# Sparse attention with split values stationary and split, scaled, turned probabilities moving

## The reference, cut to what matters

```python
o_cmp, p_cmp = nsa_compressed(q, kv[:, :, 0], kv[:, :, 1], ...)      # 31 compressed keys
o_slc = nsa_selected(q, kv[:, :, 2], kv[:, :, 3], top_i, top_ok)
o_win = nsa_window(q, kv[:, :, 4], kv[:, :, 5])
gb = jax.nn.sigmoid(g_nsa.reshape(B, S, NSA_GROUPS, NSA_HPG, 3))
y_nsa = (gb[..., 0:1] * o_cmp + gb[..., 1:2] * o_slc + gb[..., 2:3] * o_win).reshape(B, S, NSA_Q)
```

## Time and profile before

| | |
|---|---|
| median of 3 runs | 2828.78 us |
| span of the profiled execution | 2832.2 us |
| PE busy | 2781.4 us (98%) |
| DVE busy | 2007.5 us (71%) |
| ACT busy | 1158.5 us (41%) |
| POOL busy | 62.7 us (2%) |
| chain that ended last | PE 75%, DVE 20%, issue 3%, ACT 1% |
| granted PE clock | 9 or more tenths in all 40 slices |

### The profile page before, as it was taken

The page is one execution under the profiler, slowest core; times in us unless marked ns, Lnnn a source line. Parts: engine busy times, 40 slices in busy tenths (PEclk is TensorE's granted clock), DMA queues, the critical chain, the costliest instruction groups (busy, mean ns, idle before and its releaser), DMA issues.

```text
span 2832.2 us, 41533 instructions
## 1 busy us (share of the span) xinstructions
PE 2781.4 (98%) x16782; PEld 2473.6 (87%) x16782; DVE 2007.5 (71%) x2956; ACT 1158.5 (41%) x1635; POOL 62.7 (2%) x22
## 2 busy tenths in 40 slices
PE   7999999999999999999999999999999999999998
PEld 7888888888888989789898899988999888789897
DVE  4456654544658969589694797875979588669794
ACT  4333444444243424334344443432434357434342
POOL 0000011111000000000000000000000000000000
PEclk9999999999999999999999999999999999999999
DMA  7223312222533333223333233332332343123322
GB/s 221 90 78 105 112 62 84 93 81 97 184 120 98 103 107 111 104 89 105 105 105 106 79 101 109 100 114 69 109 111 93 122 171 110 60 75 107 112 95 75
DMA packets 262192, 295.39 MB, mean 104 GB/s; under 512 B 6210, under 2 KB 248018, under 8 KB 259342
## 3 DMA queue, kind: packets, MB, share of 16 engines
q1 hardware_dynamic: 257008, 281.53, 30.3%
q10 hardware_dynamic: 5022, 11.57, 1.1%
HBM read 276.30 MB, written 16.78 MB: 103 GB/s over the span
## 4 chain that ended last, share of the span: by engine, by line
PE 75%; DVE 20%; issue 3%; ACT 1%; DMA 0%; DVEq 0%; ACTq 0%; SPq 0%
PE bank L1420 13%; PE bank L1422 12%; PE bank L1421 12%; PE bank L1863 5%; PE bank L1865 5%; PE bank L1864 5%; PE bank L1694 5%; PE bank L1752 2%; DVE gate_quarters_lo L2625 2%; DVE up_quarters_lo L2625 2%; PE bank L2026 1%; PE bank L1742 1%; DVE w_lo L2121 1%; PE bank L1435 1%; PE bank L1436 1%
## 5 line engine op out<-in xcount | busy, mean ns | idle before, releaser
L2121 DVE TENSOR_TENSOR w_lo<-w_raw,w_hi 128x2048 fp32r<-128x2048 f32 (+2 forms) x140 | 306.4, 2191 | 138.9 <-ACT w_hi L831 135.7
L1420 PE MATMUL bank<-hid_hi,w_hi 128*128 128x512 f32 x880 | 343.0, 390 | 0.0
L1421 PE MATMUL bank<-hid_lo,w_hi 128*128 128x512 f32 x880 | 342.5, 389 | 0.0
L1422 PE MATMUL bank<-hid_hi,w_lo 128*128 128x512 f32 x880 | 342.4, 389 | 0.0
L831 ACT ACTIVATE w_hi<-w_raw 128x2048 fp32r<-128x2048 f32 (+2 forms) x134 | 243.0, 1820 | 240.0 <-PE bank L1422 161.3
L1420 PE MATMUL bank<-h_hi,w_hi 128*128 128x512 f32 x752 | 298.6, 397 | 3.0 <-DVE w_lo L2121 1.4
L1421 PE MATMUL bank<-h_lo,w_hi 128*128 128x512 f32 x752 | 293.0, 390 | 0.0
L1422 PE MATMUL bank<-h_hi,w_lo 128*128 128x512 f32 x752 | 292.9, 390 | 0.0
L1422 PEld LDWEIGHTS bank<-hid_hi,w_lo 128*128 128x128 f32 x880 | 165.2, 188 | 34.5
L1421 PEld LDWEIGHTS bank<-hid_lo,w_hi 128*128 128x128 f32 x880 | 165.3, 188 | 33.7
L1420 PEld LDWEIGHTS bank<-hid_hi,w_hi 128*128 128x128 f32 x880 | 165.2, 188 | 33.8
(11 more groups left out here) (465 smaller groups left out, 6962.4 us busy)
## 6 DMA issues: line engine op xcount, KB each, us to landing
w_raw<-in_ffn_w_in_dram SPq DMA_DIRECT2D x88, 1024.0 KB, 5.0
w_raw<-in_ffn_w_out_dram SPq DMA_DIRECT2D x32, 1024.0 KB, 5.2
w_raw<-in_w_in_dram SPq DMA_DIRECT2D x28, 1024.0 KB, 5.1
w_raw<-in_w_ffn_in_dram SPq DMA_DIRECT2D x22, 1024.0 KB, 5.0
w_raw<-in_ffn_w_out_dram SPq DMA_DIRECT2D x16, 768.0 KB, 4.5
w_raw<-in_conv_w_pw_dram SPq DMA_DIRECT2D x12, 1024.0 KB, 6.6
phase_taps<-in_conv_dw_phases_dram SPq DMA_DIRECT2D x10, 1152.0 KB, 7.8
w_raw<-in_w_ffn_down_dram SPq DMA_DIRECT2D x8, 1024.0 KB, 5.2
```

Source lines behind the costliest of these rows:

```text
L1420: nc.tensor.matmul(bank[b][:, 0:n], wh, xh, start=first, stop=False)
L1421: nc.tensor.matmul(bank[b][:, 0:n], wh, xl, start=False, stop=False)
L1422: ins = nc.tensor.matmul(bank[b][:, 0:n], wl, xh, start=False, stop=last)
L2121: v.tensor_tensor(w_lo[slot][:, 0:n], raw[s][:, 0:n], w_hi[slot][:, 0:n].bitcast(F32), ALU.subtract).then_inc(w_lo_ready, 1)
```

## The change

The order of steps becomes query block, branch, head, so that the 8 steps of a query block (both branches) are neighbours. PE works in 18 slots of a pair of steps (two heads): scores of pair j, `GATES_IN_SLOT[j]` gates matmuls, turn of pair j-1, weigh of pair j-2.

- Values: split in high and low parts after their projection (units 10 and 11), stored to DRAM, and loaded again for each group as `v_hl`, high and low columns side by side, 128 stationary columns.
- Probabilities: DVE scales each by the reciprocal of its sum times its gate before the transposes (`scale_step`). ACT copies the turned ones as the high part, DVE subtracts for the low part (`high_of_pair`, `low_of_pair`); the first 8 pairs (512 and 384 keys) head by head, the last 8 pair by pair.
- `weigh`: values stationary, 256 columns (two heads) of the turned high or low parts moving, fp32r. All of a query block's steps and its compressed branch add up in one bank, feature-major, with the sums of the high and of the low value columns in different partition halves.
- Compressed branch: scores from 16 matmuls of 64 columns (both key parts beside each other, no gates matmul between), scaled before its transposes; for each query block 4 transposes, a copy, and one matmul of 512 columns. Three DVE additions replace others (`cmp_add`, `cmp_parts`, `cmp_values`).
- Each block's halves are added by ACT and DVE (`move_half`, `add_halves`) and split (`y_of_block`, `y_low`). `out_step`, `y_tok`, its transposes and the multiply-adds are gone.
- ACT's high part of the second weight unit comes in slot 2, and that of the next group's first unit after the last block and `gate_evac(4)`. SP loads q and keys when the last mask step has its scores, and the values behind the group's last `add_halves`.

```diff
-STEPS = [(br, qb, hh) for br in range(2) for qb in reversed(range(TT)) for hh in range(HPG)]
+STEPS = [(br, qb, hh) for qb in reversed(range(TT)) for br in range(2) for hh in range(HPG)]
+GATES_IN_SLOT = (16, 8, 8, 8, 6, 6, 6, 6, 6, 5, 5, 5, 5, 5, 5, 5, 10, 10)
+GATE_EVAC = {2: 0, 6: 1, 10: 2, 15: 3}
+SECOND_GATE_UNIT = 2
...
+                def weigh(j):
+                    br, qb, hh = STEPS[2 * j]
+                    pe.wait_ge(s_pl, g * COPIES + (2 * j + 2 if j < NARROW else NARROW + j + 1))
+                    out_ = bank[ACC_BANK[j // 4 % 2]][:, P * hh:P * (hh + 2)]
                     for kb in range(qb + 1):
+                        keys = slice(kb * P, (kb + 1) * P)
+                        nc.tensor.matmul(out_, v_hl[:, br, kb, :], pT_hi[j % 2][:, :, keys], start=j % 4 == 0 and kb == 0, stop=False)
+                        ins = nc.tensor.matmul(out_, v_hl[:, br, kb, :], pT_lo[j % 2][:, :, keys], start=False, stop=False)
                     ins.then_inc(s_o, 1)
...
+                for j in range(PAIRS + 2):
+                    if j < PAIRS:
+                        scores(2 * j)
+                        scores(2 * j + 1)
+                    gates(GATES_IN_SLOT[j])
+                    if j == 2:
+                        pe.wait_ge(m_lo_s, 4)
+                        pe.wait_ge(vd_landed, g * 32 + (VD_LANDED + 32))
+                    if 1 <= j <= PAIRS:
+                        turn(j - 1)
+                    if j >= 2:
+                        weigh(j - 2)
+                    if j % 4 == 0 and j > 0:
+                        cmp_turn(j // 4 - 1)
+                    if j % 4 == 1 and j > 1:
+                        cmp_weigh(j // 4 - 1)
                 gates(GATE_TILES * 3 * KT)
...
+                def scale_step(i):
+                    br, qb, hh = STEPS[i]
+                    n = P * (qb + 1)
+                    dve.wait_ge(s_e, g * NS + (i + 1))
+                    link(v.reciprocal(prec[:, i:i + 1], psum_row[:, i:i + 1]))
+                    v.tensor_scalar(prob[i % 4][:, 0:n], prob[i % 4][:, 0:n], prec[:, i:i + 1], g_gate[:, qb, hh, br + 1:br + 2],
+                                    ALU.mult, ALU.mult).then_inc(s_c, 1)
...
+                for j in range(PAIRS + 2):
+                    if j < PAIRS:
+                        mask_step(2 * j)
+                        mask_step(2 * j + 1)
+                        if j == 0:
+                            cmp_add(0)
+                        scale_step(2 * j)
+                        if j == 0:
+                            cmp_add(1)
+                        scale_step(2 * j + 1)
+                    if j == 0:
+                        cmp_shift()
+                    if 1 <= j <= PAIRS:
+                        low_of_pair(j - 1)
+                    if j == 2:
+                        cmp_gain()
+                    if j == 3:
+                        cmp_scale()
+                        cmp_parts(0)
+                        cmp_values()
+                    if j == 5:
+                        compressed_keys(g + 1)
+                    if j in (6, 10, 14):
+                        cmp_parts(j // 4)
+                    if j in (7, 11, 15):
+                        add_halves(j // 4 - 1)
+                    if j in (8, 12, 16):
+                        y_low(j // 4 - 2)
```

More of the change, by code:

```diff
@@ L205 @@
 K_END = 1656
-NSA_PER = 25
+NSA_PER = 50
 class Chain:
@@ L1025, in _ @@
             act.sem_inc(gt_copied, 2)
-            for s in range(2):
-                act.sem_inc(gt_stored[s], 16)
+            act.sem_inc(gt_stored, 16)
             def q_store(n):
@@ L1097, in _ @@
                             high_in_loop(g * 2 + (U_NSA // 2 + 1), 1, 1, HALF)
[L1098 to L1102 removed]
+                move_half(TT - 1)
+                y_of_block(TT - 1)
+                gate_evac(4)
@@ L1772, in _, with turn @@
-                pe.wait_ge(q_stored, 16 * GROUPS)
-                pe.wait_ge(c_p, g + 1)
+                    out_, q = bank[S_BANK[i % len(S_BANK)]][:, 0:n], q_st[:, hh, qb * P:(qb + 1) * P]
+                    nc.tensor.matmul(out_, q, k_st[br][0][:, 0:n], start=True, stop=False)
+                    nc.tensor.matmul(out_, q, k_st[br][1][:, 0:n], start=False, stop=True).then_inc(s_s, 1)
+                def turn(j):
+                    n = P * (STEPS[2 * j][1] + 1)
+                    if j > NARROW + 1:
+                        pe.wait_ge(s_pl, g * COPIES + (NARROW + j - 1))
+                    for e in range(2):
+                        i = 2 * j + e
+                        pe.wait_ge(s_c, g * NS + (i + 1))
+                        if 1 <= j < NARROW:
+                            pe.wait_ge(s_pl, g * COPIES + (2 * (j - 1) + e + 1))
+                        if j in (NARROW, NARROW + 1) and e == 0:
+                            pe.wait_ge(s_pl, g * COPIES + (2 * NARROW - 1 + j - NARROW))
+                        b, c = (PT_BANK[e], 0) if j < NARROW else (PT_BANK[j % 2], n * e)
+                        for kb in range(n // P):
+                            ins = nc.tensor.transpose(bank[b][:, c + kb * P:c + (kb + 1) * P], prob[i % 4][:, kb * P:(kb + 1) * P], ident)
+                        ins.then_inc(s_t, 1)
@@ new lines, in cmp_turn, with cmp_weigh @@
+                def cmp_turn(k):
+                    pe.wait_ge(c_p, g * TT + (k + 1))
+                    pe.wait_ge(y_sum, g * TT + (k + 1))
+                    for hh in range(HPG):
+                        ins = nc.tensor.transpose(bank[ACC_BANK[(k + 1) % 2]][:, hh * P:(hh + 1) * P],
+                                                  c_hl[:, hh:hh + 2, :, :].rearrange("p h a n -> p (h a n)").bitcast(F32), ident)
+                    ins.then_inc(c_t, 1)
+                def cmp_weigh(k):
+                    pe.wait_ge(c_ta, g * TT + (k + 1))
+                    pe.wait_ge(vc_ready, g + (VC_READY + 1))
+                    nc.tensor.matmul(bank[ACC_BANK[k % 2]][:, :], vc_st[:, :], pT_c[:, :], start=False, stop=True).then_inc(acc_ready, 1)
@@ L1774, in _ @@
+                pe.wait_ge(q_landed, g * 16 + 16)
+                pe.wait_ge(kc_ready, g + 1)
                 for qb in range(TT):
                     for hh in range(HPG):
[L1776 to L1784 removed]
@@ L1785, in _ @@
-                ins.then_inc(c_o, 1)
-                gates(12)
-                pe.wait_ge(y_done, g + 1)
-                for t in range(2):
-                    for qb in range(TT):
-                        ins = nc.tensor.transpose(bank[6 + t][:, qb * P:(qb + 1) * P], y_tok[:, qb, t * P:(t + 1) * P], ident)
-                    ins.then_inc(y_turned, 1)
+                        c = 2 * NCP * (2 * qb + hh // 2)
+                        ins = nc.tensor.matmul(bank[PT_BANK[hh % 2]][:, c:c + 2 * NCP], q_st[:, hh, qb * P:(qb + 1) * P],
+                                               kc_st[:, :, :].rearrange("p a n -> p (a n)"), start=True, stop=True)
```

377 lines of the change are left out of this document (188 added, 189 removed).

## The result

The changed kernel takes 2860.36 us (median of 4 runs, 2859.76 to 2863.43) against 2829.32 (4 runs, 2825.6 to 2831.51): ratio 1.0114, 95% interval 1.0102 to 1.0127. It is 31 us slower, where 12 faster was forecast. The time lies outside the range; "slower" had a chance of 0.20.

A forecast was written before the change was run, and what follows sets the result against it. PE bounded the kernel before, DVE would after: 61.1 slots + 9.3 boundary, 72.3 with crossings, + 5.6 holds = 77.9 us a group; merge 12.1 us earlier, 2828.8 - 12 = 2817 us, range 2786 to 2842.

The forecast's parts named there:

- slower: Rival, chance 0.20: POOL's subtractions hold DVE for all their 13.9 us a group, giving 2850 us.
- The merge: Work behind the attention's four groups: forecast to start at 672.7 against 684.8, 12.1 us earlier.
- the boundary between groups: Behind DVE's slot 15, DVE waits for PE's gates, last turn, weighings and first scores: 9.3 us a group.
- POOL's holds: POOL's subtractions delay DVE's scalings: 3.3 us in slot 2, 1.3 in slot 7, 1.0 at group start; 5.6 a group.
- DVE's slots: DVE's masks, scalings and low parts in slots 0 to 15, plus its compressed-branch work: 61.1 us a group.
- PE's saving: Cheaper weighing 8.1, compressed output 3.1, compressed scores 1.8, dropped transposes 0.9: 13.9 us a group.
- the 77.9: Forecast time in us of one attention group: 72.3 for DVE's chain with crossings, plus 5.6 of holds.
- PE-bound: Rival, chance 0.08: DVE's waits for ACT overlap better, PE sets the time at 68.2 us a group, 2778 us.
- P: The time of one attention group in us, entering the forecast merge start as 361.1 + 4P.
- no hold: Rival, chance 0.16: POOL doesn't hold DVE's scalings, 72.3 us a group, 2794 us.
- PE's waits for POOL inside the groups: Late low weights stall PE 2.4 us a group at slot 0's gates, hidden under DVE's longer slot.
- the 0.40: Chance given to the forecast itself, 2817 us with scalings held by POOL; own range 2805 to 2824.

The follow-up runs named there:

- e1: The changed kernel with POOL's four subtractions a group cut from 2048 or 1024 columns to 64: 2814.66 us, ratio 0.9953.
- e11: e10 with DVE's program for the four groups written out instead of looped: 2809.7 us, ratio 0.9923 against the kernel before.
- e5: The changed kernel with each gates tile doing its 16 high-weight products first, then the 8 low-weight ones: 2851.25 us, ratio 1.0068.
- e13: e11 with POOL making the low weights again and no subtraction on DVE: 2826.25 us, ratio 0.9983.
- e10: The changed kernel with low-weight products last, ACT's high parts earlier, gates matmuls moved to early slots, low weights made by DVE: 2827.26 us, ratio 0.9986.
- e8: The kernel before with POOL's low-weight subtractions in the attention loop cut to 64 columns: 2827.61 us, ratio 0.9985.
- e14: The kernel before with low-weight products last in each gates tile and DVE's loop written out: 2827.96 us, ratio 0.9992.
- e9: The changed kernel with only DVE's loop over the four groups written out: 2859.02 us, ratio 1.0101.
- e3: The changed kernel with ACT making the fourth unit's and the next group's first high parts earlier, POOL kept: 2845.89 us, ratio 1.0057.
- e2: The changed kernel with the four low-weight subtractions a group made by DVE and none by POOL: 2840.39 us, ratio 1.004.

## Why the prediction was wrong

The merge was laid at 672.7 and began at 711.7, 39 us later. Experiment e1 splits that in two halves. Without POOL the forecast's own terms give 356.0 + 4 x 72.3 = 645.2; e1 has its merge at 665.7: 20.5 us. POOL was priced at 4 x 5.6 + 5.1 = 27.5 us; it costs 711.7 - 665.7 = 46.0: 18.5 us. The steps that failed in the sum are therefore two: the boundary between groups (9.3 us laid, 13.3 measured in e1) and POOL's holds (5.6 us a group laid, 10.4 to 11.1 measured). The sum went by DVE's slots and the boundary; PE's saving is in it only through the boundary.

- **PE's saving, 13.9 us a group: too large**, though the 77.9 wasn't added up from it. Adding up distances from start to start, PE's own pieces are 81.8 us of a group before and 72.7 in e1: 9.1. The price inside a run of weighings was right, 0.12 us apart, but its ends cost more (0.20 for the first), so that 80 take 12.0 us and not 9.2: 4.8 saved, not 8.1. The compressed output takes 0.42 for each matmul of 512 columns and 64 rows, not 0.23: 2.5 saved. Compressed scores and the gates between them save 4.1 (0.4 and 3.7) where 1.8 was laid. The transposes of `y_tok` save 1.0. Against that, scores are 2.4 and turns 0.8 dearer beside their new neighbours, 9.2 to 11.6 and 8.7 to 9.5; no such term was in the sum. The rival "PE-bound" laid P = 68.2, where PE's own pieces alone come to 72.7.
- **DVE's slots, 61.1 us and 0.1 a slot for crossings: right.** 434.14 to 498.67 in e1 is 64.5 against 62.7, 1.8 a group more. (70.4 and eighteen times 0.1 make 72.2, where the forecast has 72.3; this changes nothing.) Scalings took 0.546 to 0.346 us as laid.
- **The boundary, 9.3 us: wrong.** In e1 it is 13.3 (498.67 to 511.92). It was built from PE's work alone. DVE has its own chain there: 3.05 for ACT's last high part, 2.33 for its move, and 4.62 idle at the loop's jump, in e1:

```profile
501.72 0.42 DVE L2496 TENSOR_TENSOR probT_lo<-bank,probT_hi 128x256 fp32r<-128x256 f32 x1 [3.05 <-ACT probT_hi L1100]
...
504.80 0.42 DVE L2503 TENSOR_TENSOR y_half<-bank,y_half 64x256 f32<-64x256 f32 x1 [2.33 <-ACT y_half L1129]
...
511.44 0.19 DVE L2513 COPY nsa_stat<-nsa_gate 128x48 f32 x1 [4.62 <-issue]
```

  The last one no row of the kernel before could have shown: there the jump took 0.3 us. It is new with the change, and it is the term that e11 takes out.
- **Holds, 5.6 us a group: the mechanism right, the size half.** The scaling is held, as chosen, but beside POOL's short subtraction; the long ones met other instructions. The forecast put 3.3 in slot 2, and it came as 4.4 through a product of 16 columns; 1.3 in slot 7 came as 1.4; 1.0 at the group's start came as 3.0 to 3.7, since a copy of 48 columns, not listed among what can be held, stands first there; "nothing in slot 16" came as 1.6, on the low part of y. Together 10.4 to 11.1. The reciprocal that counted for "no hold" was weak evidence: at 391.73 it had 0.2 us of POOL's time left, little more than its own 0.17. The changed kernel's are better: four of one column lie well inside POOL's subtractions and take their 0.16 us.
- **PE's waits for POOL inside the groups: missing.** Only the one before the merge was priced, 5.1, and came as 5.5. The others were called hidden under DVE's longer slot. They are 20.3 us, with the lower clock behind some of them; yet taking them alone away (e5) gives 9 us, because DVE is late too, and the two windows under e1 leave next to nothing for them on top of the holds. The forecast's size for them was wrong, and its "hidden" came nearly true, in part by luck, since DVE was held for twice as long as laid.
- **The rival that came nearest** is "slower", P = 86.2 and 2850, with its point of decision at 82.4. P came at 88.8. Its reason was close (POOL costs its whole time and PE's slot 0 waits for it too); what it lacked is the boundary. Its own P was 14 us of holds on 72.3; the 88.8 came from 10.5 of holds on 78, so it came near by a wrong division.

Right as well: that PE waits for masks and low parts in the slots (6 us a group, where 8 to 10 were laid), the value split at no cost, SP's loads in time. As the forecast said it would be, it was wrong once groups were over 82 us; the 0.40 it had on 5.6 us of holds rested on counting which instruction would meet POOL, slot by slot, and a meeting is decided by ACT's high part, which ends when it will.

The cause is settled in its parts, each by its own pair: holds (e13 against e11, 16.6 us beyond DVE's own work), POOL altogether (e1, 45.7), the jump (e11 against e10, 17.6), next to nothing of them before (e8, e14). That PE's dearer scores and turns come from their neighbours is read from the distances, not tested. How the 51 us between the changed kernel and e11 divide among them is not a sum of single effects: e9 alone gives 1, e5 alone 9, e3 alone 14.5, e2 alone 20.

## What to carry to other kernels

When a change takes work off the engine that sets the time and gives it to one that had slack, list everything that the slack was hiding on the second engine (holds by a neighbour, late hand-overs) and price each as uncovered; here POOL alone was 46 us of it against a saving of 36 on PE. Look also for what the change makes new: a longer loop turned a jump of 0.3 us into one of 3 to 6. An edit that gives nothing by itself can be worth 17 us once the wait beside it is gone, so try them together before one is thrown away. Give PE the products first that need nothing late: in e14 the other order within the sum cost nothing.

## What the runs showed of the hardware

- POOL's two-source subtraction holds DVE's instructions with SBUF sources and an SBUF result, small ones too: with one source, 3.84 us for a copy of 48 columns and 1.83 for a scaling of 384; with two, 4.55 for a product of 16 and 2.05 for a low part of y. Low parts that read PSUM keep their time beside POOL (0.42 us for 256 columns), as mask steps did in the kernel before (0.69 at 391.12), and so does the reciprocal of one column (149 to 166 ns in all 128, four of them beside POOL).
- The jump back of DVE's loop takes 0.3 us with 158 instructions in a turn and 2.9 to 6.0 with 189 to 193, with a packet of the instruction queue inside each long one. The engine is idle for 0.8 to 5.6 us of it, and not at all with the loop written out.
- After a wait of 1.6 us PE's matmuls of 512 columns start 0.43 us apart for six microseconds, at a granted clock of 0.51; after one of 3.29 us elsewhere it stays at 1.00.
